# Transposing the normalised tokens by DMA from SBUF to SBUF instead of on TensorE: an encoder trunk on eight cores

## The chip, the cores and the metric

The kernel runs on all eight cores of one Trainium2 chip. Every core runs the same program on its own data and no core talks to another: four sequences of 4,096 tokens are split into halves, one half to a core. The metric is the device time of the slowest core in microseconds. A core has TensorE (PE in the profile), VectorE (DVE), ScalarE (ACT), GpSimd (POOL) and SyncE (SP), each with its own instruction stream, run in order, and 16 DMA engines that serve the queues of all of them.

## What is computed

Two layers, then a final norm. The model width is 1,024 and the feed-forward width 2,816.

```python
h = x
for i in range(2):
    hn = rms_norm(h, norm_mix_g[i])
    h = h + (even_mixer(hn, ...) if i == 0 else odd_mixer(hn, ...))
    hn = rms_norm(h, norm_ffn_g[i])
    h = h + (silu(hn @ w1) * (hn @ w3)) @ w2
return rms_norm(h, final_norm_g)

def odd_mixer(h, w_uv, v_norm_g, w_s, b_s, w_out):      # the gating layer
    z = gelu(h @ w_uv)                                  # (B, S, 2048)
    u, v = z[..., :1024], rms_norm(z[..., 1024:], v_norm_g)
    sv = w_s applied to chunks of 128 positions of v, per group, plus b_s
    return (u * sv) @ w_out
```

The even mixer (a Fourier transform beside differential attention) comes first in time and is not touched by the change.

## The kernel before

After attention, the residual of the core's 2,048 tokens stays in SBUF in float32 (`hres`, 16 tiles of 128 tokens). Everything behind it works on blocks of 1,024 tokens, that is 8 tiles. A matmul sums over the partitions, so the normalised tokens, which lie with tokens on the partitions, have to be turned: `hnT_` (SBUF, bf16) holds the 8 tiles of one block with channels on the partitions, 8 pieces of 128x128 for each tile.

The stages in order of time, with the line of their matmuls:

- Layer-0 feed-forward: up on block 0 (L1311, L1313), down on block 0 (L1334), up on block 1, down on block 1.
- Gating layer, per block: `V_stage` for each of the 8 tiles (L1473), `U_stage` for 8 channel groups (L1465), then a loop over tiles with `S_a` (a small product at L1442, scaled by ACT at L1447, added by DVE at L1453), `S_b` (DVE, L1457) and `mix_O` (L1418; its result is added to `hres` by DVE at L1420).
- Layer-1 feed-forward, like the first, and the final norm.

An up stage reads `hnT_` in two halves: the first two groups of eight matmuls read tiles 0 to 3, the next two read tiles 4 to 7, and so on. `V_stage(t)` reads tile t alone.

Each block's `hnT_` is made during the stage before it, tile by tile, in two steps. `nt_apply` (DVE, L314) writes the scaled tile into a slot `hn2` in SBUF. `nt_tr` then turns it: eight transposes on PE (L320) into one PSUM bank, and a copy of that bank into `hnT_` by `evac` (L228 on ACT or L231 on DVE, whichever has the lower running cost). So it is for 40 tiles: block 1 of the first feed-forward (in its first down stage, `hook1`), block 0 of gating (in its second down stage, `mix_hook`), block 1 of gating and block 0 of the second feed-forward (in the two gating loops), and block 1 of the second feed-forward (in its first down stage). Block 0 of the first feed-forward is turned by other code (`nt_tr_item`), which stays. The down stages rotate over three slots (`hn2[t % 3]`), the gating loops over two (`hn2[t % 2]`).

The order on each engine is the order in which Python emits the instructions; there is no scheduler. `KB` keeps for every buffer its last writer and its readers, and puts a semaphore wait in front of an instruction on the engine that issues it. SP's queue issues loads, the stores of the output and nothing else; the weights with a cast are loaded from POOL's queue.

Of the kernel before, what the change touches and what calls it, by code (L numbers as in the profile page):

```python
# [159 lines left out]
def build():  # L160
    nc = bass.Bass("TRN2", target_bir_lowering=False)
# [27 lines left out]
    es = ExitStack()  # L189
    with es:  # L190
        arena = es.enter_context(nc.sbuf_tensor("arena", [128, 207 * 512], BF16))
        psum = es.enter_context(nc.psum_tensor("psum", [128, 4096], F32))
        k = KB(nc, es)

        def view(off_kib, shape, dt):
            esz = 2 if dt == BF16 else 4
            n = 1
            for s_ in shape[1:]:
                n *= s_
            o = int(off_kib * 512)  # L200
            a = arena[:, o:o + n * esz // 2]
            if dt == F32:
                a = a.bitcast(F32)
            if len(shape) == 3:
                a = a.rearrange("p (a b) -> p a b", a=shape[1])
            elif len(shape) == 4:
                a = a.rearrange("p (a b c) -> p a b c", a=shape[1], b=shape[2])
            return a
# [4 lines left out]
        def bank_bf(i):  # L213
            return psum[:, i * 512:(i + 1) * 512].bitcast(BF16)

        bankB = [Buf("bank%d" % i) for i in range(8)]
        bank_rr = [0]

        def next_bank():
            i = bank_rr[0] % 8  # L220
            bank_rr[0] += 1
            return i

        def evac(out, in_, reads, writes, scale=None, n=512, eng=None):
            e = eng or k.pick(0.25 + n / 1000.0)
            if e == "act":
                if scale is None:
                    return k.op("act", lambda: nc.scalar.copy(out=out, in_=in_), reads, writes)  # L228
                return k.op("act", lambda: nc.scalar.activation(out=out, in_=in_, func=AF.Copy, scale=float(scale)), reads, writes)
            if scale is None:  # L230
                return k.op("dve", lambda: nc.vector.tensor_copy(out=out, in_=in_), reads, writes)  # L231
            return k.op("dve", lambda: nc.vector.tensor_scalar(out=out, in0=in_, scalar1=float(scale), scalar2=None, op0=ALU.mult), reads, writes)

        ident = view(200, [128, 128], BF16)
# [10 lines left out]
        identB = Buf("ident")  # L245
# [15 lines left out]
             reads=[identB], writes=[identB])  # L261
# [50 lines left out]
        def nt_apply(stY, i, tile, gv, gvB, slot, slotB):  # L312
            st, Y = stY
            k.op("dve", lambda: nc.vector.scalar_tensor_tensor(out=slot, in0=hres[:, tile, :], scalar=Y[:, i:i + 1], in1=gv, op0=ALU.mult, op1=ALU.mult),  # L314
                 reads=list(hB[tile]) + [st[4], gvB], writes=[slotB])

        def nt_tr(slot, slotB, t, hnT_, hnTB_):
            bi = next_bank()
            bb = bank_bf(bi)
            k.group("pe", [(lambda kk=kk: nc.tensor.transpose(out=bb[:, kk * 128:(kk + 1) * 128], in_=slot[:, kk * 128:(kk + 1) * 128], identity=ident))  # L320
                           for kk in range(8)], reads=[slotB, identB], writes=[bankB[bi]])
            evac(hnT_[:, :, t * 128:(t + 1) * 128], bb.rearrange("p (a b) -> p a b", a=8), [bankB[bi]], [hnTB_[t]], n=1024)

        eps_t = view(205.75, [128, 2], F32)
        epsB = Buf("eps")
# [822 lines left out]
        hnT_ = view(84, [128, 8, 1024], BF16)  # L1148
# [128 lines left out]
        def ffn(l, up_hook=None, pre_down1=None, down1_hook=None, warm_pairs=1):  # L1277
# [70 lines left out]
            def hook1(t):  # L1348
                nt_apply(box["st"], t, 8 + t, gvF, NX["gvFB"], hn2[t % 3], hn2B[t % 3])
                if t >= 1:  # L1350
                    nt_tr(hn2[(t - 1) % 3], hn2B[(t - 1) % 3], t - 1, hnT_, hnTB_)

            up(0, up_hook0)
            down(0, hook1)
            nt_tr(hn2[7 % 3], hn2B[7 % 3], 7, hnT_, hnTB_)
            up(1)
            pre_down1()
# [12 lines left out]
        def mix_hook(t):  # L1370
            nt_apply(MX["st"], t, t, gvF, NX["gvFB"], hn2[t % 3], NX["hn2B"][t % 3])
            if t >= 1:
                nt_tr(hn2[(t - 1) % 3], NX["hn2B"][(t - 1) % 3], t - 1, hnT_, NX["hnTB"])
# [49 lines left out]
        hnTB_, hn2B = NX["hnTB"], NX["hn2B"]  # L1423
# [224 lines left out]
```

How the kernel before makes its waits and increments, by code:

```python
    def _wait(self, e, evs):  # L75
        best = {}
        for ev in evs:
            if ev is None:
                continue
            sem, val, key = ev
            if self.seen[e].get(key, 0) >= val:
                continue
            if key not in best or best[key][1] < val:
                best[key] = ev
        for key, (sem, val, _) in best.items():
            self.eng[e].wait_ge(sem, val)
            self.seen[e][key] = val
# [23 lines left out]
    def _signal(self, e, inst):  # L111
        self.ecnt[e] += 1
        inst.then_inc(self.esem[e], 1)
        return (self.esem[e], self.ecnt[e], e)
# [17 lines left out]
    def dma(self, q, out, in_, reads=(), writes=(), sembuf=None, waw=True):  # L132
        deps = self._deps(reads, writes)
        if not waw:
            ws = {id(b.w) for b in writes if b.w is not None}
            deps = [e for e in deps if id(e) not in ws]
        self._wait(q, deps)
        sb = sembuf if sembuf is not None else (writes[0] if writes else reads[0])
        if sb.sem is None:
            sb.key = "d%d" % len(self.dbufs)
            sb.sem = self.es.enter_context(self.nc.semaphore("s_" + sb.key))
            self.dbufs.append(sb)
        sb.cnt += 16
        self.eng[q].dma_start(out=out, in_=in_).then_inc(sb.sem, 16)
        ev = (sb.sem, sb.cnt, sb.key)
        self._commit(ev, reads, writes)
        return ev
```

## Time and profile before

| | |
|---|---|
| time, median of 3 runs | 1960.21 us (1960.11 to 1961.51) |
| the profiled execution's own time | 1971.49 us |
| its span on the profiled core (core 3, the slowest) | 1970.2 us |
| spans of the other cores | 1950.8 to 1965.8 us |
| mean granted TensorE clock, core 3 | 0.971 (others up to 0.985) |
| PE, ACT, DVE, POOL busy | 95%, 46%, 42%, 8% of the span |

The span runs from the first to the last instruction of one core; the time is measured around it. The profile is of one execution, which was 11.3 us (0.6%) longer than the median of the runs. Busy time of PE counts pipelined matmuls, so it doesn't tell PE at its peak; the start times do.

### The profile page before, as it was taken

Reading aid. Unit: us, or ns where it says so; the run is one execution under the profiler, and the core shown is the slowest. Engines: PE = TensorE matmul, PEld = TensorE weight load, DVE = VectorE, ACT = ScalarE, POOL = GpSimd, SP = SyncE. Lnnn points to the kernel's source line nnn. Section 1 sums busy time; section 2 is a strip of 40 time slices with the busy share of each in tenths; the row PEclk is TensorE's granted clock in tenths of the full one; section 3 lists DMA queues with packets and bytes.
Section 4 is the critical chain, followed back from the end, with each engine's and each line's share of the span. In section 5 each row is a group of like instructions: output and inputs, shape, how many; then the busy total and the mean of one; then the engine's idle time right before and its main releaser. Section 6 shows DMA issues by size and latency. Waiting matters only on the chain.

```text
span 1970.2 us, 36548 instructions; the slowest of 8 cores (1950.8 to 1970.2 us)
## 1 busy us (share of the span) xinstructions
PE 1874.4 (95%) x12869; PEld 1016.3 (52%) x12869; DVE 821.4 (42%) x1746; ACT 896.9 (46%) x1209; POOL 149.3 (8%) x176
## 2 busy tenths in 40 slices
PE   4899999999998998999999999999999999999997
PEld 3576555566655665644444444444444444444443
DVE  3564345545555667742222211323545222221145
ACT  3563778888887887813200112045652131011121
POOL 0000000000000000011200111012031221001100
PEclk7788999999999999999999999999999999999999
DMA  9311421000315000378730564232033876036512
GB/s 229 119 65 42 90 87 18 19 7 7 104 38 180 14 24 19 52 106 112 107 46 11 72 79 52 34 59 50 12 44 44 115 110 86 1 43 86 76 70 103
DMA packets 137056, 129.51 MB, mean 66 GB/s; under 512 B 9777, under 2 KB 116529, under 8 KB 136882
## 3 DMA queue, kind: packets, MB, share of 16 engines
q0 software_dynamic: 112544, 69.22, 26.7%
q1 hardware_dynamic: 24338, 57.96, 8.9%
q8 instruction: 112, 1.84, 0.4%
q14 instruction: 62, 0.51, 0.1%
HBM read 187.97 MB, written 8.39 MB: 100 GB/s over the span
## 4 chain that ended last, share of the span: by engine, by line
PE 84%; ACT 5%; DVE 5%; issue 4%; DMA 1%; DVEq 0%; SPq 0%; ACTq 0%
PE psum L1311 15%; PE psum L1313 15%; PE psum L1334 15%; PE psum L1072 10%; PE psum L1031 6%; PE psum L1473 3%; PE psum L1465 3%; PE psum L916 2%; PE psum L1418 2%; ACT arena L1055 2%; PE psum L826 2%; PE psum L530 1%; PE psum L764 1%; PE psum L508 1%; PE psum L840 1%
## 5 line engine op out<-in xcount | busy, mean ns | idle before, releaser
L1311 PE MATMUL psum<-arena 128*128 128x512 bf16 x1408 | 332.6, 379 | 0.0
L1313 PE MATMUL psum<-arena 128*128 128x512 bf16 x1408 | 332.6, 379 | 0.0
L1317 ACT ACTIVATE arena<-psum 128x512 f32<-128x512 f32 x176 | 104.9, 597 | 498.5 <-PE psum L1311 482.8
L1072 PE MATMUL psum<-arena 128*128 128x129 bf16 x4096 | 318.0, 222 | 5.5 <-DVE arena L1091 3.4
L1318 DVE TENSOR_TENSOR arena<-psum,arena 128x512 bf16<-128x512 f32 x176 | 121.2, 691 | 452.7 <-PE psum L1313 438.0
L1334 PE MATMUL psum<-arena 128*128 128x512 bf16 x1408 | 309.3, 380 | 0.0
L1072 PEld LDWEIGHTS psum<-arena 128*128 128x128 bf16 x4096 | 252.6, 98 | 104.7 <-issue 77.9
L1053 ACT ACTIVATE arena<-psum 128x1024 bf16<-128x1024 f32 x244 | 243.2, 1024 | 68.9 <-PE psum L1032 62.5
L1313 PEld LDWEIGHTS psum<-arena 128*128 128x128 bf16 x1408 | 137.8, 98 | 166.1
L1311 PEld LDWEIGHTS psum<-arena 128*128 128x128 bf16 x1408 | 137.5, 98 | 163.2
L1334 PEld LDWEIGHTS psum<-arena 128*128 128x128 bf16 x1408 | 137.3, 98 | 162.1 <-issue 1.7
L1031 PE MATMUL psum<-arena 64*128 64x512 bf16 x512 | 177.2, 382 | 28.7 <-ACT arena L1055 11.8
L1055 ACT ACTIVATE arena<-psum,arena 128x1024 bf16<-128x1024 f32 x168 | 180.2, 1114 | 39.7 <-PE psum L1032 37.6
L1032 PE MATMUL psum<-arena 64*128 64x512 bf16 x512 | 180.0, 388 | 0.0
L144 POOL DMA_DIRECT2D arena<-w x132 | 101.8, 776 | 1011.2 <-PE psum L1311 571.9
L1059 DVE TENSOR_TENSOR arena<-arena 128x1024 bf16<-128x1024 f32 x100 | 122.3, 1223 | 55.2 <-ACT arena L1058 19.7
L277 ACT ACTIVATE arena<-arena 128x1024 bf16<-128x1024 f32 (+1 forms) x104 | 110.0, 1058 | 69.2 <-DVE arena L1336 60.9
L228 ACT COPY arena<-psum 128x1024 bf16<-128x1024 bf16 x36 | 36.6, 1015 | 213.9 <-PE psum L320 202.4
L1336 DVE TENSOR_TENSOR arena<-psum,arena 128x512 f32<-128x512 f32 x64 | 44.1, 690 | 175.3 <-PE psum L1334 175.3
L1058 ACT ACTIVATE arena<-psum 128x1024 f32<-128x1024 f32 x100 | 102.1, 1021 | 0.3 <-DVE arena L1059 0.3
L1031 PEld LDWEIGHTS psum<-arena 64*128 64x128 bf16 x512 | 44.0, 93 | 101.5 <-issue 73.8
L231 DVE CAST arena<-psum 128x512 bf16<-128x512 f32 x52 | 41.1, 791 | 82.3 <-PE psum L826 25.8
(124 smaller groups left out, 1682.6 us busy)
## 6 DMA issues: line engine op xcount, KB each, us to landing
arena<-w POOLq DMA_DIRECT2D x88, 512.0 KB, 8.3
arena<-x SPq DMA_DIRECT2D x48, 512.0 KB, 8.6
arena<-w POOLq DMA_DIRECT2D x44, 256.0 KB, 9.8
arena<-dft SPq DMA_DIRECT2D x8, 1024.0 KB, 6.8
out<-arena SPq DMA_DIRECT2D x16, 512.0 KB, 2.7
arena<-wown SPq DMA_DIRECT2D x8, 576.0 KB, 4.4
arena<-wfo SPq DMA_DIRECT2D x8, 512.0 KB, 8.8
arena<-w_uv POOLq DMA_DIRECT2D x4, 1024.0 KB, 15.3
```

What stands on the lines that cost most here:

```text
L277: k.op("act", lambda: nc.scalar.activation(out=junk, in_=src, func=AF.Square, accum_out=st[0][:, col:col + 1]), reads=srcB, writes=[st[4], ...
L1031: k.group("pe", [lambda: nc.tensor.matmul(Lq[i][:, 0:512], lhsT=KTh[h][0:64, ks], rhs=QTh[h][0:64, qs], start=True, stop=True), lambda: nc ...
L1032: lambda: nc.tensor.matmul(Lq[i][:, 512:1024], lhsT=KTh[h][64:128, ks], rhs=QTh[h][64:128, qs], start=True, stop=True)],
L1053: k.op("act", lambda: nc.scalar.activation(out=Pb[pb], in_=Lq[i], func=AF.Exp), reads=LBs, writes=[PB[pb]])
L1055: k.op("act", lambda: nc.scalar.activation(out=Pb[pb], in_=Lq[i], func=AF.Exp, bias=bconst[:, col:col + 1], scale=1.0), reads=LBs + [bcons ...
L1059: k.op("dve", lambda: nc.vector.tensor_tensor(out=Pb[pb].rearrange("p (m q) -> p m q", m=2), in0=Tn, in1=eb.unsqueeze(1).to_broadcast([128 ...
L1072: return lambda: nc.tensor.matmul(psum[:, c0:c0 + 129], lhsT=P_[:, idx * 128:(idx + 1) * 128], rhs=Vp[h // 2][:, kt, h % 2, 0:129], start= ...
L1311: k.group("pe", [(lambda kk=kk: nc.tensor.matmul(bank(b1), lhsT=w13[sl][:, 0, kk, jj * 128:(jj + 1) * 128], rhs=hnT_[:, kk, ts], start=(kk ...
L1313: k.group("pe", [(lambda kk=kk: nc.tensor.matmul(bank(b3), lhsT=w13[sl][:, 1, kk, jj * 128:(jj + 1) * 128], rhs=hnT_[:, kk, ts], start=(kk ...
L1317: k.op("act", lambda: nc.scalar.activation(out=sil[ss_], in_=bank(b1), func=AF.Silu), reads=[bankB[b1]], writes=[silB[ss_]])
L1318: k.op("dve", lambda: nc.vector.tensor_tensor(out=GT[:, j, ts], in0=bank(b3), in1=sil[ss_], op=ALU.mult), reads=[bankB[b3], silB[ss_]], wr ...
L1334: k.group("pe", [(lambda j=j: nc.tensor.matmul(bank(bi), lhsT=GT[:, j, t * 128:(t + 1) * 128], rhs=W2[j][:, hs_], start=(j == 0), stop=(j ...
```

## The change

`nt_tr` no longer uses PE, a PSUM bank or an evacuation. A new helper, `dma_tr`, issues eight transposing DMAs from SP's queue, one for each 128x128 piece, straight from the slot to `hnT_`. It waits once, ahead of the first of the eight: for the scaled tile, and for the last readers and the last writer of that tile of `hnT_`. All eight raise one semaphore that belongs to the tile of `hnT_`. The slot is free for the next `nt_apply` only when all eight have landed. Everything else is as before, but `bank_rr`, the counter of PSUM banks, advances one less for each tile.

```diff
--- before.py
+++ after.py
@@ -314,12 +314,19 @@
             k.op("dve", lambda: nc.vector.scalar_tensor_tensor(out=slot, in0=hres[:, tile, :], scalar=Y[:, i:i + 1], in1=gv, op0=ALU.mult, op1=ALU.mult),
                  reads=list(hB[tile]) + [st[4], gvB], writes=[slotB])
 
+        def dma_tr(dsts, srcs, slotB, dstB):
+            k._wait("sp", k._deps([slotB], [dstB]))
+            if dstB.sem is None:
+                dstB.key = "d%d" % len(k.dbufs)
+                dstB.sem = es.enter_context(nc.semaphore("s_" + dstB.key))
+                k.dbufs.append(dstB)
+            for o_, i_ in zip(dsts, srcs):
+                dstB.cnt += 16
+                nc.sync.dma_start(out=o_, in_=i_, transpose=True).then_inc(dstB.sem, 16)
+            k._commit((dstB.sem, dstB.cnt, dstB.key), [slotB], [dstB])
+
         def nt_tr(slot, slotB, t, hnT_, hnTB_):
-            bi = next_bank()
-            bb = bank_bf(bi)
-            k.group("pe", [(lambda kk=kk: nc.tensor.transpose(out=bb[:, kk * 128:(kk + 1) * 128], in_=slot[:, kk * 128:(kk + 1) * 128], identity=ident))
-                           for kk in range(8)], reads=[slotB, identB], writes=[bankB[bi]])
-            evac(hnT_[:, :, t * 128:(t + 1) * 128], bb.rearrange("p (a b) -> p a b", a=8), [bankB[bi]], [hnTB_[t]], n=1024)
+            dma_tr([hnT_[:, kk, t * 128:(t + 1) * 128] for kk in range(8)], [slot[:, kk * 128:(kk + 1) * 128] for kk in range(8)], slotB, hnTB_[t])
 
         eps_t = view(205.75, [128, 2], F32)
         epsB = Buf("eps")
```

The order of instructions shows what now waits for what. First DVE, in the gating loop of block 0, for tiles 1 to 3, before the change (L314 is `nt_apply`, L1453 and L1457 are `S_a` and `S_b`, L1420 the residual add, L231 the evacuation; `e_pe` is PE's semaphore):

```order
L314 SCALAR_TENSOR_TENSOR arena<-arena 128x1024
L1453 TENSOR_TENSOR arena<-arena 128x8x128 [waits e_act]
L1457 TENSOR_TENSOR arena<-arena 128x8x128 [waits e_dve]
L314 SCALAR_TENSOR_TENSOR arena<-arena 128x1024 [waits e_pe]
L1453 TENSOR_TENSOR arena<-arena 128x8x128 [waits e_act]
L1457 TENSOR_TENSOR arena<-arena 128x8x128 [waits e_dve]
L1420 TENSOR_TENSOR arena<-psum,arena 128x512 [waits e_pe] x2
L231 COPY arena<-psum 128x8x128 [waits e_pe]
L314 SCALAR_TENSOR_TENSOR arena<-arena 128x1024
```

The same place of the changed kernel, whose lines are numbered seven higher there (`s_d54` is the semaphore of tile 0 of `hnT_`, `s_d55` that of tile 1, and so on to `s_d61`):

```order
L314 SCALAR_TENSOR_TENSOR arena<-arena 128x1024 [waits s_d61]
L1460 TENSOR_TENSOR arena<-arena 128x8x128 [waits e_act]
L1464 TENSOR_TENSOR arena<-arena 128x8x128 [waits e_dve]
L314 SCALAR_TENSOR_TENSOR arena<-arena 128x1024 [waits s_d54]
L1460 TENSOR_TENSOR arena<-arena 128x8x128 [waits e_act]
L1464 TENSOR_TENSOR arena<-arena 128x8x128 [waits e_dve]
L1427 TENSOR_TENSOR arena<-psum,arena 128x512 [waits e_pe] x2
L314 SCALAR_TENSOR_TENSOR arena<-arena 128x1024 [waits s_d55]
```

The copy is gone, and each `nt_apply` of this loop now waits on DVE for the transposes of the tile two before it, which had the same slot.

Then SP's queue from the end of the layer-0 feed-forward into the gating layer, before:

```order
L144 DMA arena<-gvecs 128x1024 [waits s_d48,e_dve]
L144 DMA arena<-wsT 128x1024 [waits e_act,e_pe,s_d53]
L144 DMA arena<-bs 128x1024 [waits s_d25,s_d26,s_d53]
L144 DMA arena<-gvecs 128x8x1
L144 DMA arena<-gvecs 128x1024 [waits s_d48,e_dve]
```

And in the changed kernel, from the last tile of that feed-forward's second down stage on:

```order
L325 DMA_TRANSPOSE arena<-arena 128x128 [waits e_dve,s_d61]
L325 DMA_TRANSPOSE arena<-arena 128x128 x7
L144 DMA arena<-wsT 128x1024 [waits e_act,s_d53,e_pe]
L144 DMA arena<-bs 128x1024 [waits s_d25,s_d26,s_d53]
L144 DMA arena<-gvecs 128x8x1
L325 DMA_TRANSPOSE arena<-arena 128x128 [waits e_dve,s_d54,e_pe]
L325 DMA_TRANSPOSE arena<-arena 128x128 x7
L325 DMA_TRANSPOSE arena<-arena 128x128 [waits e_dve,s_d55]
L325 DMA_TRANSPOSE arena<-arena 128x128 x7
```

Three loads of the gating layer stand behind the transposes of the stage before it, and 64 transposes stand between them and the next load of a gain vector.

## Rows read from the trace of the kernel before

**Rows 1.** The page: span, busy time, PE's granted clock in 40 slices, chain by engine.

```profile
span 1970.2 us, 36548 instructions; the slowest of 8 cores (1950.8 to 1970.2 us)
...
PE 1874.4 (95%) x12869; PEld 1016.3 (52%) x12869; DVE 821.4 (42%) x1746; ACT 896.9 (46%) x1209; POOL 149.3 (8%) x176
...
PEclk7788999999999999999999999999999999999999
...
PE 84%; ACT 5%; DVE 5%; issue 4%; DMA 1%; DVEq 0%; SPq 0%; ACTq 0%
```

**Rows 2.** Timeline of PE, layer-0 feed-forward, first down stage: start us, us, what.

```profile
993.29 9.66 PE L1334 MATMUL psum<-arena 128*128 128x512 bf16 x44
1002.79 0.61 PE L320 MATMUL psum<-arena 128*128 128x128 bf16 x8
1003.24 9.66 PE L1334 MATMUL psum<-arena 128*128 128x512 bf16 x44
...
1072.39 0.61 PE L320 MATMUL psum<-arena 128*128 128x128 bf16 x8
1072.84 1.89 PE L1311 MATMUL psum<-arena 128*128 128x512 bf16 x8
...
1076.29 1.89 PE L1311 MATMUL psum<-arena 128*128 128x512 bf16 x8
```

**Rows 3.** The same timeline, layer-0 second down stage and the start of gating.

```profile
1224.79 9.66 PE L1334 MATMUL psum<-arena 128*128 128x512 bf16 x44
1238.88 1.01 PE L320 MATMUL psum<-arena 128*128 128x128 bf16 x8 [4.44 <-DVE arena L314]
1239.69 10.95 PE L1334 MATMUL psum<-arena 128*128 128x512 bf16 x44
...
1310.13 0.61 PE L320 MATMUL psum<-arena 128*128 128x128 bf16 x8
1310.58 27.79 PE L1473 MATMUL psum<-arena 128*128 128x512 bf16 x128
```

**Rows 4.** Timeline of all engines in the gating stage, first half of the tokens.

```profile
1362.82 3.62 PE L1465 MATMUL psum<-arena 128*128 128x512 bf16 x16
...
1397.68 1.01 ACT L228 COPY arena<-psum 128x1024 bf16<-128x1024 bf16 x1
1397.81 1.28 DVE L314 SCALAR_TENSOR_TENSOR arena<-arena 128x1024 bf16<-128x1024 f32 x1
...
1404.62 0.61 PE L320 MATMUL psum<-arena 128*128 128x128 bf16 x8
```

**Rows 5.** Timeline of PE in the gating stage, second half.

```profile
1457.31 3.62 PE L1465 MATMUL psum<-arena 128*128 128x512 bf16 x16
...
1498.62 0.61 PE L320 MATMUL psum<-arena 128*128 128x128 bf16 x8
1499.07 1.89 PE L1311 MATMUL psum<-arena 128*128 128x512 bf16 x8
```

**Rows 6.** First gating loop: length, busy PE, PEld, DVE, ACT, POOL, clock, DMA share, GB/s.

```profile
1366.70:1405.10 38.40, 35.40 (x245) 18.52 (x243) 36.34 (x42) 25.56 (x72) 11.99 (x5) 1.00 0.04 15
```

**Rows 7.** Timeline of all engines, gating, second half: the last scaled tile.

```profile
1491.82 1.27 DVE L314 SCALAR_TENSOR_TENSOR arena<-arena 128x1024 bf16<-128x1024 f32 x1
```

**Rows 8.** Timeline of DVE at the first down stage.

```profile
994.24 1.28 DVE L314 SCALAR_TENSOR_TENSOR arena<-arena 128x1024 bf16<-128x1024 f32 x1
```

**Rows 9.** SP's issues, its queue's timeline: start us, us of issuing.

```profile
1310.95 0.33 SPq L144 DMA_DIRECT2D arena<-bs  x1
1311.33 0.42 SPq L144 DMA_DIRECT2D arena<-gvecs  x1
```

**Rows 10.** DMA of 1318 to 1330 us: packets, MB, share of 16 engines.

```profile
DMA packets 2486, 1.62 MB, mean 135 GB/s; under 512 B 910, under 2 KB 2486, under 8 KB 2486
...
q1 hardware_dynamic: 894, 0.00, 9.7%
```

**Rows 11.** The page: DMA issues, KB, median us from issue to landing.

```profile
out<-arena SPq DMA_DIRECT2D x16, 512.0 KB, 2.7
```

## The prediction

> **What bounds the kernel now.** I read the page first: PE is busy for 95% of the span, its granted clock is in the top tenth from the fifth slice of forty on, and the chain that ended last is 84% PE [rows 1]. So an instruction taken from PE's stream saves its time unless something else comes late in its place. Then PE's timeline, stage by stage. In a down stage the 44 matmuls of a tile and eight transposes follow each other without a gap: the transposes begin at 1002.79 us, the next tile's matmuls at 1003.24, so they cost 0.45 us a tile, and the last group of eight borders directly on the next stage's first matmul, at 1072.84 [rows 2]. There is one wait for this work: in the second down stage PE stands 4.44 us until DVE has scaled the first tile. The transposes behind that wait take 1.01 us where others take 0.61, and the tile after them 10.95 us where others take 9.66 [rows 3]. The gating loops are different. From 1366.7 to 1405.1 us PE is busy for 35.4 of 38.4 us, but DVE for 36.3 [rows 6]: whatever holds DVE there holds the loop. DMA's share in that stretch is 0.04, so the transposes would meet next to no other traffic.
>
> **What it removes.** 40 tiles with 0.45 us of PE each: 18.0 us. The wait of 4.44 us, and what followed it, 0.40 + 1.29 us: 6.1 us; the down stage no longer needs that tile, and the DMAs have the rest of the stage for it. Together 24.1 us. The 40 evacuations, about 1 us each on ACT [rows 4], come off engines that mostly wait for PE; in the gating loops they may help DVE a little, which I cost at nothing beyond the 0.45. SP waits for scaled tiles in the middle of its queue, ahead of three loads for the gating layer. These were issued at about 1311 us [rows 9] and serve the loop behind 1362.82 [rows 4]: 50 us of cover, so nothing. Without that cover, each microsecond of lateness would be one of the gating loop's.
>
> **What it adds.** 320 transposing DMAs of 32 KB, 64 in each of five stretches. The trace has no transposing DMA, so I bound one from both sides. From below: SP issues DMAs back to back every 0.38 us (1310.95, then 1311.33) [rows 9], so eight take 3.0 us at least. From above: a transpose scatters 2-byte elements. In pieces of one element that would be 16,384 pieces. The smallest pieces in the trace are those of the transposed gain vector, 4 bytes each: 894 packets in the 12 us from 1318 us took 9.7% of 16 engines, 18.6 us, so 20.8 ns each [rows 10] (beside other traffic, so perhaps less alone). 16,384 of them are 341 us of engine time, 21 us over 16 engines. In pieces of whole rows, 256 bytes, it would be only 128 pieces, under 0.2 us, and SP's issue would be the limit. The ends are far apart and no row is near. I take the middle in ratio between 128 and 16,384 pieces, some 1,450, rounded to 1,024 pieces of 32 bytes: 21.3 us of engine time, 1.33 us over 16 engines. It is an estimate. A tile then takes T = 8 x 1.33 = 10.64 us, one transpose after the other.
>
> The Trainium skill ("VectorE: DVE Perf Modes", The three transpose paths) gives 1,309 ns for a 128x128 bf16 transpose by DMA and 390 ns for one on TensorE, and by its DMA figure a tile would be 10.5 us and the sum below some 6 us lower. Its figure for TensorE, eight times 390 ns, is not what this trace shows: eight take 0.45 us in the stream, so by its comparison DMA loses less than it does here.
>
> **What on the path waits for it.** To land I add 2 us to the chain of transposes: a 512 KB store lands 2.7 us after its issue [rows 11], and part of that is data. Then, for any T:
>
> A, the first down stages of both feed-forwards. Scaling of the first tile ends at 994.24 + 1.28 = 995.5 us [rows 8], the eighth tile lands at 995.5 + 8T + 2. The next up stage starts after 8 x 9.5 = 76.0 us, at 1069.3, and needs tiles 4 to 7 for its third group, 3.45 us later (1076.29 less 1072.84) [rows 2], at 1072.7. Wait: 8T - 75.2 = 9.9 us, twice: 19.8.
>
> B, the second down stage. The chain starts at 1238.5 and ends at 1240.5 + 8T = 1325.6. `V_stage` of tile 7 begins at 1224.8 [rows 3] + 76.0 + 7 x 3.45 (16 matmuls of the same size as in two groups of an up stage) = 1324.9. Wait: 0.7.
>
> M, the gating loops. The first tiles of `hnT_` are free when the first half of the last `U_stage` is done, 1.7 us behind 1362.82. Now the slots bind: `nt_apply` of tile 7 needs tile 5 landed, six tiles from there: 1364.6 + 6T + 2 = 1430.4. In the trace it starts at 1397.81 [rows 4], 1394.6 without the seven groups of transposes before it. DVE stands in front of `nt_apply`, and behind it stand the adds that make `yT`, on which `mix_O` waits. Late by 35.8 us. In the second loop, from 1457.31 [rows 5] and 1491.82 [rows 7], by 36.2. Together 72.0.
>
> U, the up stage behind the second loop. From the last `nt_apply` to its start are 6.8 us (1491.82 to 1498.62), to its third group 3.45 more; the eighth tile lands 8T + 2 after the loop's start against 6T + 2 for `nt_apply`. Wait: 2T - 10.3 = 11.0.
>
> Clock: behind the one wait of 4.4 us PE lost 1.7 us. I count that five times, behind the long waits that end these stretches: 8.5.
>
> Sum: 19.8 + 0.7 + 72.0 + 11.0 + 8.5 - 24.1 = 87.9 us. The profiled execution took 1971.5 us, its span 1970.2; it would take 2059. The median of the runs stands 11.3 us lower, so I predict 1960.2 + 88 = 2048 us.
>
> **The rivals.** Every wait is a straight line in T, so they differ in what one transpose takes. Faster: SP's issue is the limit. At 0.38 us T is 3.0, all four waits are zero and 24.1 us are gained: 1936. At 0.75 us T is 6.0, only M is left, 8 us and 8.4 for the two loops, and U, 1.7: 1954. This is the case if the pieces are whole rows of 256 bytes, 128 of them. For it speaks that the DMAs are nearly idle in these stretches; against it, that a row of the source ends in 128 partitions. The Trainium skill ("Advanced Engine Details and Errata", X-Bar Transpose (TRN2)) says that transposing DMAs are as fast as regular ones, 350 to 400 GB/s: 32 KB in 0.1 us, which would make this rival true. Chance 0.2.
>
> No change: the sum is zero near T = 6.4, 0.80 us for one, where M takes 21 us and U 2.5. Chance 0.05.
>
> Much slower: above 2 us for one, from smaller pieces or from long work of SP's queue for each instruction, neither of which the trace can exclude. At exactly 2 us T is 16: A 105.6, B 43.6, M 136.4, U 21.7, clock 8.5, less 24.1, is 292 us: 2252. At the upper bound of 21 us for one it would be thousands. Chance 0.17.
>
> My forecast, between 0.8 and 2 us: 1964 to 2252, chance 0.58.
>
> **How the numbers follow.** The predicted time is that of the likeliest case at its likeliest size. The range leaves out only the much slower case: 1936 to 2252. A measurement of this kernel can tell a change of about 0.2%, 4 us, from none. Faster 0.2, same 0.05, slower 0.75.
>
> **What would show it.** In the profile after, line 320's matmuls are gone and the eight transposes of a tile land T after its scaling; the landing times and the spacing of SP's issues give T directly. In the down stages PE should run tile after tile with no break, as now. In the gating loops DVE should stand idle in front of `nt_apply` for DMA, with the loops about 74 us long instead of 38. At the start of the up stages PE should wait 8 to 11 us at its third group. The granted clock should dip there. The prediction is wrong if landings of consecutive tiles stand less than 6 us apart, or if transposes of one queue overlap so that T is set by the issue; also if weight loads, not transposes, are what comes late.

## The result, and the profile after

The change makes the kernel slower. The median of five runs is 2073.79 us against 1961.51 us of before; the ratio is 1.0538, 95% interval 1.0492 to 1.0584. Executions in which all cores of a die ran long at a lower granted clock (one of these five, 2247.40 us) are left out of this ratio and of all that follow. Of the other four, one took 2045.93 us and three 2072 to 2074 us; in each of the three, two neighbouring cores end 26 to 30 us behind the median of the other six. The profiled one is of the latter kind: cores 0 and 1 end at 2071.7 and 2072.5 us, the others at 2033 to 2051.

The page of the changed kernel (core 1), against [rows 1]:

```profile
span 2072.5 us, 36290 instructions; the slowest of 8 cores (2033.1 to 2072.5 us)
...
PE 1900.8 (92%) x12549; PEld 1004.1 (48%) x12549; DVE 809.1 (39%) x1726; ACT 875.9 (42%) x1189; POOL 148.3 (7%) x176
...
PEclk7899999999999999999999999988978999988899
...
PE 66%; SPq 18%; ACT 5%; issue 5%; DVE 4%; DMA 2%; DVEq 0%; ACTq 0%
SPq L325 18%; PE psum L1318 15%; PE psum L1320 15%; PE psum L1079 9%; PE psum L1038 6%; PE psum L1341 4%; PE psum L1472 3%; PE psum L923 2%; ACT arena L1062 2%; PE psum L1480 2%; PE psum L833 2%; PE psum L771 1%; PE psum L537 1%; PE psum L847 1%; DMA arena<-arena 1%
```

SP's queue, which had no share of the chain before, now has 18% of it, all at line 325, the transposing DMA. All of them together (the columns are duration in ns, minimum, median and maximum):

```profile
L325 SPq DMA_TRANSPOSE arena<-arena x320: 1077/1202/2412, 982.8 to 1804.0; - x160
...
  DVE arena L314: 63.4, 12
  PE psum L1318: 21.2, 3
  PE psum L1480: 8.6, 1
...
DMA to landing us min/median/max: 2.2/2.3/11.8
```

An issue takes SP's queue 1.20 us at the median and never under 1.08, and the transposed piece lands 2.3 us after its issue began, so 1.1 us after SP let go of it. The chain of issues sets the pace: in the first gating loop SP issues its 64 without a break. That stretch in SP's timeline, and the DMA share over it:

```profile
1359.18 81.03 SPq L325 DMA_TRANSPOSE arena<-arena  x64
1440.32 0.50 SPq L144 DMA_DIRECT2D arena<-gvecs  x1
```

```profile
DMA packets 10085, 2.13 MB, mean 26 GB/s; under 512 B 10080, under 2 KB 10080, under 8 KB 10080
...
q1 hardware_dynamic: 10080, 2.07, 12.3%
```

81.03 us for 64 is 1.27 us each, T = 10.1 us. The 16 DMA engines are busy for 12.3% of that time. The packets are 160 for each transpose, of 205 bytes on average: in the trace they are 128 rows of 256 bytes and 32 packets of 4 bytes, and not 1,024 pieces of 32 bytes. The DMAs of this one queue also overlap: an issue begins 1.27 us after the one before, while that one's piece is still on its way, 2.3 us.

PE's timeline shows the price. The next lines answer to [rows 2] and [rows 3]:

```profile
1066.35 3.57 PE L1318 MATMUL psum<-arena 128*128 128x512 bf16 x8 [6.36 <-DMA arena<-arena]
```

```profile
1217.77 76.14 PE L1341 MATMUL psum<-arena 128*128 128x512 bf16 x352
1293.74 24.34 PE L1480 MATMUL psum<-arena 128*128 128x512 bf16 x112
1326.65 6.10 PE L1480 MATMUL psum<-arena 128*128 128x512 bf16 x16 [8.57 <-DMA arena<-arena]
...
1362.41 3.61 PE L1425 MATMUL psum<-arena 128*128 128x512 bf16 x16 [0.69 <-ACT arena L1454]
...
1366.93 3.61 PE L1425 MATMUL psum<-arena 128*128 128x512 bf16 x16 [0.47 <-ACT arena L1454]
...
1375.38 5.30 PE L1425 MATMUL psum<-arena 128*128 128x512 bf16 x16 [4.38 <-DVE arena L1427]
...
1385.35 5.30 PE L1425 MATMUL psum<-arena 128*128 128x512 bf16 x16 [4.22 <-DVE arena L1427]
...
1424.95 6.44 PE L1425 MATMUL psum<-arena 128*128 128x512 bf16 x16 [5.77 <-DVE arena L1464]
```

A down stage is now one block of 352 matmuls in 76.1 us, without a break: the transposes are gone from it, and so is the wait of 4.44 us. But PE waits 6.36 us for tiles 4 to 7 in the up stage behind it, 8.57 us for tile 7 at the end of `V_stage`, and from the third tile of the gating loop on about 4 us a tile; `mix_O` starts every 10 us instead of every 5. DVE in that loop:

```profile
1370.67 1.28 DVE L314 SCALAR_TENSOR_TENSOR arena<-arena 128x1024 bf16<-128x1024 f32 x1 [4.09 <-DMA arena<-arena]
...
1371.87 1.22 DVE L1460 TENSOR_TENSOR arena<-arena 128x1024 bf16<-128x1024 f32 x1
...
1380.63 1.28 DVE L314 SCALAR_TENSOR_TENSOR arena<-arena 128x1024 bf16<-128x1024 f32 x1 [4.91 <-DMA arena<-arena]
...
1381.84 1.22 DVE L1460 TENSOR_TENSOR arena<-arena 128x1024 bf16<-128x1024 f32 x1
```

`nt_apply` (L314) waits for a DMA, and the adds of `S_a` stand behind it.

The loop pays for these waits a second time. The 16 matmuls of `mix_O` take 5.0 to 6.4 us behind them, where they took 3.6 before. The window of the first loop on core 1 (the columns are the window, its length, busy PE, PEld, DVE, ACT and POOL, the granted clock, DMA's share, GB/s) has a granted clock of 0.78, where before it was 1.00 [rows 6]:

```profile
1362.40:1431.20 68.80, 43.91 (x168) 17.88 (x169) 33.11 (x36) 22.24 (x67) 10.24 (x5) 0.78 0.13 27
```

Stage by stage on one core, from the start times in PE's timeline (core 1 in both):

| stage | before, us | after, us | of it a wait for DMA |
|---|---|---|---|
| down, layer 0, block 0 | 79.5 | 76.0 | |
| up, block 1 | 152.0 | 161.4 | 6.4 |
| down, block 1 | 85.6 | 76.0 | |
| V_stage, gating block 0 | 27.6 | 38.8 | 8.6 |
| gating loop, block 0 | 37.0 | 68.8 | through DVE |
| gating loop, block 1 | 36.8 | 69.1 | through DVE |
| up, layer 1, block 0 | 152.0 | 162.3 | 7.6 |
| down, block 0 | 79.5 | 76.0 | |
| up, block 1 | 152.0 | 189.0 (core 3: 160.6) | 7.2 (6.7) |

From the first up stage on, the stages that are left out are equal to 0.2 us. The last row is where the two slow cores lose their 27 us. Windows of that stage on core 1 and on core 3 (columns as above):

```profile
1850.00:1870.00 20.00, 20.00 (x78) 8.30 (x77) 2.80 (x5) 2.99 (x5) 2.63 (x3) 0.81 0.43 52
```

```profile
1850.00:1870.00 20.00, 20.00 (x94) 9.05 (x93) 4.04 (x6) 3.59 (x6) 1.75 (x2) 1.00 0.78 95
```

Both have PE busy throughout, but core 1 is granted 0.81 of the clock where core 3 has all of it.

Such a stretch is in the trace of before too, in the even mixer, which the change doesn't touch. The same columns on core 1 and on core 3 of before:

```profile
95.00:190.00 95.00, 88.63 (x734) 64.36 (x733) 58.64 (x134) 48.73 (x79) 3.50 (x4) 0.96 0.24 67
```

```profile
95.00:190.00 95.00, 94.08 (x678) 66.92 (x677) 55.46 (x122) 42.92 (x72) 0.00 (x0) 0.81 0.15 48
```

There it is cores 2 and 3 that are granted 0.81. They begin the first up stage at 829.9 and 834.2 us, the other six at 814.2 to 824.2, and they end last; so the profiled execution of before, 11.3 us longer than the median, was long for the same reason. A pair of neighbouring cores at 0.81 needs no transposing DMA.

### The profile page after: what moved, and what is told of

Its sections match the earlier page's. It is cut to its first block, busy times and chain, and to the rows that moved or that the text cites. A ratio compares the mean times of both kernels' runs of the same rounds, so it can differ in the third digit from the quotient of the medians.

```text
span 2072.5 us, 36290 instructions; the slowest of 8 cores (2033.1 to 2072.5 us)
## 1 busy us (share of the span) xinstructions
PE 1900.8 (92%) x12549; PEld 1004.1 (48%) x12549; DVE 809.1 (39%) x1726; ACT 875.9 (42%) x1189; POOL 148.3 (7%) x176
## 4 chain that ended last, share of the span: by engine, by line
PE 66%; SPq 18%; ACT 5%; issue 5%; DVE 4%; DMA 2%; DVEq 0%; ACTq 0%
SPq L325 18%; PE psum L1318 15%; PE psum L1320 15%; PE psum L1079 9%; PE psum L1038 6%; PE psum L1341 4%; PE psum L1472 3%; PE psum L923 2%; ACT arena L1062 2%; PE psum L1480 2%; PE psum L833 2%; PE psum L771 1%; PE psum L537 1%; PE psum L847 1%; DMA arena<-arena 1%
## 5 line engine op out<-in xcount | busy, mean ns | idle before, releaser
L1318 PE MATMUL psum<-arena 128*128 128x512 bf16 x1408 | 352.0, 395 | 21.2 <-DMA arena<-arena 21.2
L1320 PE MATMUL psum<-arena 128*128 128x512 bf16 x1408 | 349.3, 393 | 0.0
L1341 PE MATMUL psum<-arena 128*128 128x512 bf16 x1408 | 304.5, 379 | 0.0
L1079 PEld LDWEIGHTS psum<-arena 128*128 128x128 bf16 x4096 | 252.2, 98 | 104.4 <-issue 77.6
L1318 PEld LDWEIGHTS psum<-arena 128*128 128x128 bf16 x1408 | 141.7, 101 | 199.6 <-issue 74.0
L1320 PEld LDWEIGHTS psum<-arena 128*128 128x128 bf16 x1408 | 141.7, 101 | 179.4 <-issue 50.8
L1341 PEld LDWEIGHTS psum<-arena 128*128 128x128 bf16 x1408 | 137.8, 98 | 166.1
L1425 PE MATMUL psum<-arena 128*128 128x512 bf16 x256 | 82.9, 496 | 52.1 <-DVE arena L1427 33.1
L314 DVE SCALAR_TENSOR_TENSOR arena<-arena 128x1024 bf16<-128x1024 f32 x48 | 63.1, 1315 | 63.6 <-DMA arena<-arena 63.4
## 6 DMA issues: line engine op xcount, KB each, us to landing
arena<-w POOLq DMA_DIRECT2D x44, 256.0 KB, 10.1
```

The source lines that it names most:

```text
L1079: return lambda: nc.tensor.matmul(psum[:, c0:c0 + 129], lhsT=P_[:, idx * 128:(idx + 1) * 128], rhs=Vp[h // 2][:, kt, h % 2, 0:129], start= ...
L1318: k.group("pe", [(lambda kk=kk: nc.tensor.matmul(bank(b1), lhsT=w13[sl][:, 0, kk, jj * 128:(jj + 1) * 128], rhs=hnT_[:, kk, ts], start=(kk ...
L1320: k.group("pe", [(lambda kk=kk: nc.tensor.matmul(bank(b3), lhsT=w13[sl][:, 1, kk, jj * 128:(jj + 1) * 128], rhs=hnT_[:, kk, ts], start=(kk ...
L1341: k.group("pe", [(lambda j=j: nc.tensor.matmul(bank(bi), lhsT=GT[:, j, t * 128:(t + 1) * 128], rhs=W2[j][:, hs_], start=(j == 0), stop=(j ...
```

## The experiments

Eight kernels were run, all derived from the changed one. My theory before them: a transposing DMA costs SP's queue about 1.25 us for each instruction, and that alone sets T. The rivals were that the DMA engines or the traffic of the weights set it, and that an issue costs in proportion to its data.

**Only the down stages by DMA.** A switch in `nt_tr`:

```diff
-        def nt_tr(slot, slotB, t, hnT_, hnTB_):
-            dma_tr(...)
+        def nt_tr(slot, slotB, t, hnT_, hnTB_, where="down"):
+            if where == "down":
+                dma_tr(...)
+                return
+            # the transposes on PE and the evacuation of before
```

> Transposes by DMA only for the 24 tiles of the down stages; the 16 tiles of the gating loops are turned by TensorE as before the change. My theory: SP's queue takes some 1.25 us for each transposing DMA, so the gating loops alone cost 32 us each, and the down stages nearly break even. From the changed kernel's stage lengths against those of before: down stages -3.6, -9.6, -3.6 us, what follows each +9.4, +11.2, +10.8: +15 us on 1961, so 1976 (about 26 more if one pair of cores keeps a lower clock through the last up stage, 2002). The gating loops last 37 us again. Rival, the loads of weights that the transposes collide with carry the loss: then this kernel keeps most of it, 2040 or more.

Measured 1973.72 us, ratio 1.0067 (1.0050 to 1.0085). The gating loops last 36.7 us again, the up stages behind the chains 162.6 and 162.8. The waits of the change behind the down stages are all there, that of `V_stage` in PE's timeline of core 0:

```profile
1327.40 5.51 PE L1487 MATMUL psum<-arena 128*128 128x512 bf16 x16 [8.64 <-DMA arena<-arena]
```

So the down stages cost 13 us net, near the 15 expected. The rival is out: this kernel has all the collisions of the down stages with weight loads, and it keeps only 13 us of the loss.

**Only the gating loops by DMA.** The same switch, `where == "gate"`.

> The reverse: transposes by DMA only for the 16 tiles of the two gating loops, all down stages as before the change. My theory: +31.8, +32.4 for the loops, +10.4 for the up stage behind the second: 1961 + 75 = 2036. If the two parts add, the gains and losses of this kernel and of the one with the down stages alone sum to the loss of the whole change (+85 without the low clock of one pair of cores in the last up stage). Rival: the parts interact (the low clock that follows one wait is carried into the next stage), then the sum differs by over 10 us.

Only two of six executions count, of 2037.27 and 2060.70 us, so the interval of the ratio is wide, 1.0349 to 1.0555 (1.0452). The profile is of an execution that doesn't count, of 2129.08 us; on its core 0, where the other stages from the first up stage on are as long as before, the loops last 69.2 and 69.4 us and the up stage behind them 162.5. That is +32.2, +32.6 and +10.5, 75.3 us. With the 13 of the other part the sum is 88; the change itself has 84.4 in its execution without slow cores (2045.93 less 1961.51). The parts add, to within 4 us.

**Plain copies in their place.** `transpose=True` is left out, so what goes into `hnT_` isn't transposed; waits and places stay.

> All 320 DMAs stay in their place with their waits, but copy the 128x128 pieces as they lie instead of transposing them, so the output leaves the transposition out. Theory: what takes 1.2 us is SP's queue working out a transposing DMA; a plain one takes 0.38 us there, T is 3 to 4 us, no wait is left: 1961 - 24 = 1937, gating loops of 33 to 35 us. Rival: any DMA between two places of SBUF in 256-byte rows is as slow, or the landing time of 2.3 us binds: then 2040 to 2074 as with the change.

Measured 1943.65 us, ratio 0.9919 (0.9900 to 0.9939). SP's issue of these DMAs, and what waited:

```profile
L325 SPq DMA_DIRECT2D arena<-arena x320: 464/586/1894, 983.8 to 1699.0; - x160
...
  DVE arena L314: 5.6, 6
...
DMA to landing us min/median/max: 1.7/1.8/5.6
```

A plain DMA of the same shape takes SP 0.59 us, half of a transposing one (not the 0.38 that I expected, the distance of two issues in [rows 9]), and the time is 7 us above the 1937 expected. With 0.61 us from issue to issue T is 4.9 us, no up stage is longer than before, and the gating loops last 36.2 and 37.8 us where T just touches them. It moves as many rows of 256 bytes as the change does, and behind the issue a piece lands after 1.2 us here and 1.1 us there. So it is the issue that costs, not the pieces or the landing.

**One DMA for a whole tile.** The destination has three dimensions, so that one instruction turns 128 partitions x 1,024 into eight pieces of 128x128:

```diff
-            dma_tr([hnT_[:, kk, t * 128:(t + 1) * 128] for kk in range(8)], [slot[:, kk * 128:(kk + 1) * 128] for kk in range(8)], slotB, hnTB_[t])
+            dma_tr([hnT_[:, :, t * 128:(t + 1) * 128]], [slot], slotB, hnTB_[t])
```

> One transposing DMA for a whole tile (128 partitions x 1024, written as 8 pieces of 128x128) instead of eight, 40 in all. Theory A, SP's queue has a fixed cost for each instruction: the issue takes 1.2 to 2 us for a tile, T is 2 to 4 us, no wait is left, 1937. Theory B, SP's queue works in proportion to the size (it makes the descriptors of each 128x128 piece one after the other): the issue takes 8 to 10 us for a tile and the time stays at 2045 to 2074.

Measured 1936.83 us, ratio 0.9881 (0.9864 to 0.9898): 1.2% faster than before the change. Theory A holds:

```profile
L325 SPq DMA_TRANSPOSE arena<-arena x40: 1217/1217/1977, 983.7 to 1688.6; - x40
...
DMA to landing us min/median/max: 3.0/3.1/9.3
```

One issue of eight times the data takes 1.22 us, and the whole tile lands 3.1 us after it began. Nothing waits for a transpose any more. The page (core 5):

```profile
span 1935.4 us, 36010 instructions; the slowest of 8 cores (1928.5 to 1935.4 us)
...
PE 1837.1 (95%) x12549; PEld 989.3 (51%) x12549; DVE 807.3 (42%) x1726; ACT 875.7 (45%) x1189; POOL 144.5 (7%) x176
...
PEclk7899999999999999999999999999999999999999
...
PE 81%; DVE 6%; ACT 5%; issue 5%; DMA 1%; DVEq 0%; SPq 0%; ACTq 0%
```

PE is busy for 1837.1 us. The 1874.4 us of [rows 1] are those of a core with a stretch at 0.81; core 1 of before, which had none, was busy for 1856.8, so some 20 us are gone. SP is out of the chain, and the granted clock is in its top tenth from the third slice on. The gating loops last 33.9 and 34.1 us, the down stages 76.0, all others as before: 3 x 3.5, 6.1 more in the second down stage, 3.1 and 2.7 in the loops make 22.4 us, of the 24 measured.

**Four DMAs for a tile**, each of 128 partitions x 256 (`hnT_[:, 2 * kk:2 * kk + 2, ...]` from `slot[:, kk * 256:(kk + 1) * 256]`).

> Four transposing DMAs for a tile, each of 128 partitions x 256 (two pieces of 128x128), in all five stages. Theory: SP's queue takes 1.22 us for each instruction whatever its size, so T is 4.9 us, just under the pace of the gating loops of before (5.0): loops of 35 to 38 us, no wait for transposes at the up stages, 1938 to 1943. Rival, a cost in proportion to the data once instructions are shorter: T stays near 10 and the time at 2045.

Measured 1947.41 us (1940.98 to 1948.24), ratio 0.9925 (0.9906 to 0.9943), 4 us above the upper end expected.

```profile
L325 SPq DMA_TRANSPOSE arena<-arena x160: 1167/1247/2207, 984.3 to 1702.5; - x160
...
  DVE arena L314: 6.8, 5
...
DMA to landing us min/median/max: 2.3/2.4/8.1
```

The issue is 1.25 us again. With 1.26 us from issue to issue and the wait for the next scaled tile, a tile takes 5.2 us at best. The up stages wait for nothing; the gating loops last 39.7 and 37.4 us on core 6, the first over the 35 to 38 expected: DVE still waits 6.8 us in them, and PE is granted 0.96 and 0.95 of its clock. At the loop's own pace T is at its threshold.

**Sixteen DMAs for a tile**, each of 64 partitions x 128.

```diff
+            dma_tr([hnT_[:, kk, t * 128 + 64 * h:t * 128 + 64 * h + 64] for kk in range(8) for h in range(2)],
+                   [slot[64 * h:64 * h + 64, kk * 128:kk * 128 + 128] for kk in range(8) for h in range(2)], slotB, hnTB_[t])
```

> Sixteen transposing DMAs for a tile, each of 64 partitions x 128. Theory of a fixed 1.2 us for each instruction: T is 19 to 20 us; by the straight lines of the prediction (A 8T - 75.2 twice, B 8T - 84.4, M 6T - 28 twice, U 2T - 10.3) with T = 19.5: 162 + 72 + 178 + 29 - 24 = 416, and some 30 of lower clock: 2370 to 2420. Rival, a cost in proportion to the rows: each takes 0.6 us, T stays at 10 and the time at 2045 to 2075.

Measured 2439.85 us, ratio 1.2443 (1.2417 to 1.2470).

```profile
L325 SPq DMA_TRANSPOSE arena<-arena x640: 1088/1228/2540, 983.3 to 2198.0; - x160
...
  DVE arena L314: 394.1, 25
  PE psum L1319: 203.1, 5
  POOL arena L144: 58.6, 1
```

```profile
1150.31 3.57 PE L1319 MATMUL psum<-arena 128*128 128x512 bf16 x8 [75.86 <-DMA arena<-arena]
```

Half the data, the same 1.23 us. The time lies 20 us above the upper end of what I expected. The straight lines left out that at this T the three slots of the down stages bind too (the first lasts 88 us instead of 76), `V_stage` of the second gating block waits too (39.7 us instead of 27.6), and a load from POOL's queue waits 58.6 us for a transpose. PE waits 203.1 us for transposes in the up stages, DVE 394.1 us in front of `nt_apply`; tiles 4 to 7 of the first chain alone hold PE for 75.86 us.

**DMA for six of eight tiles in the down stages only.** `where == "down" and t < 6`, PE for the rest.

> Eight transposing DMAs for a tile, but only for tiles 0 to 5 of the three down stages; tiles 6 and 7 and both gating loops are turned by TensorE. Theory: the loss of the down stages is only that a chain of 10 us a tile ends too late, and the gain is 0.45 us for each tile taken from TensorE and the wait of 6.1 us in the second down stage. Without the last two tiles nothing is late: 1961 - 18 x 0.45 - 6.1 = 1947. Rival: the transposes cost the down stages something beside lateness (PSUM banks, DMA traffic of the weights): then 1955 or more.

Measured 1947.10 us, ratio 0.9930 (0.9909 to 0.9952): as expected to 0.1 us. The down stages last 76.9 us, every up stage 152, `V_stage` 27.6. So in the down stages the slow issues do harm only by the late end of the chain.

**Work for PE in the place of the wait.** Behind the second group of each up stage but the first, 28 matmuls into a bank that nobody reads:

```diff
+                            if jp == 0 and jj == 0 and tc == 1 and (l, blk) != (0, 0):
+                                bw = next_bank()
+                                next_bank()
+                                k.group("pe", [(lambda kk=kk: nc.tensor.matmul(bank(bw), lhsT=w13[sl][:, 0, kk % 8, 0:128], rhs=hnT_[:, kk % 8, 0:512], start=True, stop=True))
+                                               for kk in range(28)], reads=[NX["w13B"][sl][0]] + hnTB_[0:4], writes=[bankB[bw]])
```

> The changed kernel with eight transposing DMAs for a tile, plus 28 matmuls of no use (0.22 us each at full clock, 6 us) on TensorE ahead of the third group of each up stage that waits for tiles 4 to 7, into a bank that nobody reads. Theory: what an up stage loses beyond its wait (161 to 164 us with waits of 6.4 to 7.7 us, against 152) is TensorE's lower granted clock behind the wait, and so is the last up stage of 189 us on one pair of cores. Then the up stages behind a wait fall to 158 to 162 us and the 189 us don't occur: 2035 to 2046. Rival: the excess, the 189 us above all, comes by chance or from the gating loops and not from that wait: then up stages as before or up to 6 us longer, and a pair of cores at 2070 in some executions again.

Measured 2048.22 us (2046.01 to 2063.68), ratio 1.0463 (1.0419 to 1.0506), 2 us above the upper end expected. Core 1, the stage that had a wait of 6.36 us and lasted 161.4:

```profile
1055.80 6.21 PE L1319 MATMUL psum<-arena 128*128 128x512 bf16 x28
1063.83 1.89 PE L1323 MATMUL psum<-arena 128*128 128x512 bf16 x8 [1.82 <-DMA arena<-arena]
1065.55 1.89 PE L1325 MATMUL psum<-arena 128*128 128x512 bf16 x8
```

A short wait of 1.82 us is left, the next groups run at 1.73 us each at once (in the changed kernel the first group behind the wait takes 3.57 us), and the stage lasts 160.0: 152.0 + 6.2 + 1.8. So the 3 us that such a stage lost beyond its wait on this core were the clock (its mean over the stage is 1.00 here, 0.97 in the changed kernel). On cores 0 and 2 the stages last 160 to 163 us, so not all of it is won.

The stretch at 0.81 is another matter. The profiled execution, the longest of the four, has it twice: on cores 2 and 3 in the even mixer, as in the trace of before, so that they begin the first down stage at 1001.4 and 997.1 us instead of 976 to 981; and on cores 0 and 1 in the last down stage, which lasts 100.9 and 97.5 us instead of 87.6. Core 0 there:

```profile
1975.00:2045.00 70.00, 69.56 (x264) 28.99 (x267) 35.70 (x98) 12.65 (x22) 0.00 (x0) 0.81 0.23 91
```

It begins 14 us into that stage, over 160 us behind the last wait for a DMA. So the dummy work wins back most of the short dip. The long stretch comes even where no wait is near, which speaks for the rival: it comes by chance or from something else than that wait.

## Why the prediction came out right, and where its working was wrong

The forecast was 88 us slower, 1936 to 2252; measured are 84 us in the execution without two slow cores and 112 us at the median. The direction, the places that wait and the straight lines in T were right. The mechanism that set T was not: the prediction named as a sign of being wrong "if transposes of one queue overlap so that T is set by the issue", and that is what the trace shows. That the wrong mechanism gave a T within 5% of the measured one was luck, and that the errors of the terms below cancel in the sum was luck again. Term by term, on core 1:

- **What it removes, 24.1 us.** Right. The kernel with one DMA for a tile shows it by itself: 24.2 us between the medians (1960.98 of before in those runs), 22.4 of them found in the stages.
- **The price of a transpose, 1.33 us, T = 10.64.** The size was near, 1.27 us and 10.1, but the step behind it was wrong. I set it by pieces on the DMA engines, 1,024 of 32 bytes, a middle between two ends with no row near it. The trace shows rows of 256 bytes and engines busy for an eighth of the time. I had the rows in the faster rival, and from them I would have concluded that SP's issue binds, at 0.38 us. What I missed is that the issue itself is dear: 1.2 us for a transposing DMA, 0.59 for a plain one of the same shape. The bound from below, taken from the issue of a large load, was the wrong row for both.
- **A, 9.9 us twice.** 6.4 and 7.2; 8T - 75.2 is 5.6 with T = 10.1 and 7.3 with the 10.3 from tile to tile in the first of these chains. Over the eight cores the waits are 6.2 to 8.6 and 6.7 to 10.2.
- **B, 0.7 us.** 8.6. I had the chain's start and pace; the last piece lands 11.8 us after its issue (the longest landing of line 325), where I had allowed 2. The landings of the 48 transposes that begin from 1231 to 1293 us, and of the 16 behind them:

```profile
DMA to landing us min/median/max: 2.2/2.3/4.4
```

```profile
DMA to landing us min/median/max: 2.2/7.6/11.8
```

Meanwhile POOL's loads of the gating layer's weights keep the DMA engines busy (ten of them in the DMA view from 1231 to 1330 us; the columns are KB each and median us to landing). Packets of POOL's queue take 6.3% of the 16 engines' time up to 1293 us, and 93.9% from 1306 to 1327.

```profile
arena<-w_uv POOLq DMA_DIRECT2D x2, 1024.0 KB, 15.3
arena<-w_out POOLq DMA_DIRECT2D x8, 256.0 KB, 23.4
```

This is the most mis-sized of the waits: a landing of some 2 us held only where no bulk load ran. That the loads are the cause is argued from their place; no run moved them.
- **M, 72.0 us.** The loops grew by 31.8 and 32.3 us; with the 7.2 us of transposes taken from them that is 71.3. The place was right, the agreement luck. What M prices is how late the last `nt_apply` of each loop starts: counted as in the prediction, 32.4 and 33.1 us, 65.5 together, which is twice 6T - 28 with T = 10.1 (65.2). The other 5.8 us come behind that `nt_apply`, where the last `mix_O` takes 6.4 us instead of 3.6 at a lower granted clock. T was too long, the clock in the loops was too cheap, and the two cancel.
- **U, 11.0 us.** 7.6 (7.5 to 9.3 over the cores); 2T - 10.3 with T = 10.1 is 9.9.
- **Clock, 8.5 us.** 3.0, 2.6 and 2.7 us beyond the wait in the first up stage, `V_stage` and the up stage behind gating, 1.9 on core 3 in the last, and the 5.8 us of the loops: 16.0, nearly twice what I had. On two cores the last up stage lost 30 us instead, at a granted clock of 0.81. That is the difference between 2046 and 2074. I missed that the trace of before has such a stretch, on its cores 2 and 3; I took its 11.3 us as a plain offset, and nothing of the kind is in the sum.

The rule of the Trainium skill ("VectorE: DVE Perf Modes", The three transpose paths), 1,309 ns for a 128x128 transpose by DMA, is close to the 1.27 us from issue to issue here, but it reads as a price of 128x128 elements, and the runs show a price of an instruction: 64x128, 128x128, 128x256 and 128x1024 take 1.23, 1.20, 1.25 and 1.22 us. The rule of the rival (the Trainium skill, "Advanced Engine Details and Errata", X-Bar Transpose (TRN2)), that they are as fast as regular DMAs, doesn't hold for the issue (1.20 us against 0.59 for a plain one of the same shape) and nearly holds for what follows it (1.1 and 1.2 us). Its 350 to 400 GB/s are not reached here even by one instruction for a whole tile: 256 KB land in 3.1 us, 85 GB/s from issue to landing, where a plain store of 512 KB takes 2.7.

What stays open is what starts a stretch at 0.81, and why on two neighbouring cores. The long waits are not needed for it: it is in the trace of before, and in the kernel with the dummy work it begins in the middle of a stage. They don't suffice either: in the profiled execution all eight cores wait 6.7 to 10.2 us in the last up stage and only cores 0 and 1 get it, and the kernel with only the down stages by DMA waits 8.9 us there on core 0 and shows it on no core. It came out in three of four executions of the changed kernel and in one of two with only the gating loops by DMA (cores 4 and 5 at 2058 and 2059 us, the others at 2024 to 2034). Of before, the profiled execution has it, and none of the fifteen others that count took more than 1964 us. So the change seems to make it more frequent, but four executions are few, and the cause of it stays unknown.

## What to carry to other kernels

An operation that moves to a DMA queue moves its cost to the issuing engine's sequencer: count the instructions there before the bytes, and try first whether one instruction can carry more. The same edit with one transposing DMA for a tile instead of eight is 1.2% faster than the kernel before, where the edit as made is 5.4% slower. And where a chain of transfers feeds a stage, its last link decides: leaving the last two tiles of eight on TensorE turned the down stages from a loss of 13 us into a gain of 14.

## What the runs showed of the hardware that I had not expected

- SP's issue of a transposing DMA takes 1.2 us whatever its size, from 64x128 to 128x1024 elements of 2 bytes; that of a plain SBUF-to-SBUF copy of 128x128 takes 0.59 us, and that of a 512 KB load 0.33 us in [rows 9] (1.19 us for the same load of the changed kernel, right behind the transposes).
- By its packets a transposing DMA moves rows of 256 bytes: 160 packets for a piece of 128x128, 128 of 256 bytes and 32 of 4.
- Two neighbouring cores can be granted 0.81 of TensorE's clock together for a long stretch, with PE busy, while the others are at or near full clock: cores 2 and 3 of before from 92 to 194 us, cores 0 and 1 of the changed kernel from 1815 to 1974 us. It adds some 10 us to the time of the chip in the first case and 27 in the second, since the slowest core counts.
- With a wait of 3 to 6 us in nearly every tile of the gating loop, the granted clock is 0.78 over the loop, and the same 16 matmuls take 5.0 to 6.4 us instead of 3.6.
